# Attention on one core: the fourth query's block moved ahead of the first scores, one root for all queries' sums, and another order of output blocks and score groups

## What is computed

```python
def second_block(x, ...):
    h = rmsnorm(x, g_norm1[l]) * (1.0 + sc1) + sh1
    proj = h @ w_in[l]                                  # q 512, k 128, v 128, z 1024 columns
    q = apply_axial_rope(rmsnorm(q.reshape(B, S, 8, 64), g_q[l]), cos, sin)
    k = apply_axial_rope(rmsnorm(k.reshape(B, S, 2, 64), g_k[l]), cos, sin)
    s = einsum('bqkgd,bskd->bkgqs', q, k) / 8           # 8 query heads on 2 key heads
    attn = einsum('bkgqs,bskd->bqkgd', softmax(s), v)
    tok = chunked_token_mlp(z, g_tok_v[l], w_s[l], b_s[l])
    mixed = concatenate([rmsnorm(attn, g_attn_out[l]), rmsnorm(tok, g_tok_out[l])])
    x = x + gt1 * (mixed @ w_out[l])
```

## Time and profile before

| | |
|---|---|
| median of 3 runs | 737.29 us (737.09 to 738.39) |
| the profiled execution | 737.35 us, its span 735.4 us |
| PE busy | 721.1 us, 98% |
| DVE, ACT, POOL busy | 586.2, 469.0, 150.4 us |
| chain that ended last | PE 88%, DVE 4%, ACT 3% |

### The profile page before, as it was taken

One profiled execution on the slowest core, in us unless ns is written; L12 is line 12 of the kernel. 1 busy time (PEld: TensorE's weight loads), 2 busy tenths in 40 slices (PEclk: granted clock), 3 DMA queues, 4 the chain that ended last, 5 costly groups with the idle time before them and its releaser, 6 DMA issues.

```text
span 735.4 us, 14308 instructions
## 1 busy us (share of the span) xinstructions
PE 721.1 (98%) x5265; PEld 663.8 (90%) x5265; DVE 586.2 (80%) x880; ACT 469.0 (64%) x793; POOL 150.4 (20%) x151
## 2 busy tenths in 40 slices
PE   8999999999999999999999999999999999999996
PEld 7999999999999799888988877997889999999895
DVE  7999989855976587876686998998698889866667
ACT  7778775678765474555545548778686555555565
POOL 5000000021333042342232320010003121333330
PEclk9999999999999999999999999999999999999999
DMA  7664443354555859898787892963337775666551
GB/s 280 184 190 159 157 133 121 117 164 144 188 176 181 302 191 408 295 306 304 244 286 255 265 319 73 340 230 119 106 116 244 240 234 179 189 188 195 172 172 58
DMA packets 48082, 151.20 MB, mean 206 GB/s; under 512 B 9600, under 2 KB 11656, under 8 KB 48024
## 3 DMA queue, kind: packets, MB, share of 16 engines
q1 hardware_dynamic: 46184, 146.62, 60.0%
q10 hardware_dynamic: 1840, 3.80, 1.4%
HBM read 147.73 MB, written 1.06 MB: 202 GB/s over the span
## 4 chain that ended last, share of the span: by engine, by line
PE 88%; DVE 4%; ACT 3%; DMA 1%; issue 1%; SPq 1%; ACTq 0%; DVEq 0%
PE ps L881 30%; PE ps L538 21%; PE ps L814 21%; PE ps L1127 1%; PE ps L1187 1%; ACT wh L1241 1%; DVE wl L1856 1%; PE ps L669 1%; PE ps L1076 1%; DMA qrot<-qg 1%; PE ps L688 1%; PE ps L595 1%; DMA vtk<-in_x 1%; PE ps L954 1%; SPq L484 1%
## 5 line engine op out<-in xcount | busy, mean ns | idle before, releaser
L1856 DVE TENSOR_TENSOR wl<-raw,wh 128x1024 fp32r<-128x1024 f32 x220 | 282.6, 1291 | 78.9 <-ACT wh L1241 77.2
L1241 ACT ACTIVATE wh<-raw 128x1024 fp32r<-128x1024 f32 x220 | 231.5, 1055 | 62.4 <-PE ps L814 47.5
L881 PE MATMUL ps<-xh,wh 128*128 128x256 f32 x656 | 184.8, 282 | 0.0
L881 PE MATMUL ps<-xh,wl 128*128 128x256 f32 x656 | 183.8, 280 | 0.0
L881 PE MATMUL ps<-xl,wh 128*128 128x256 f32 x656 | 183.8, 280 | 0.0
L881 PEld LDWEIGHTS ps<-xh,wh 128*128 128x128 f32 x656 | 123.6, 188 | 3.8 <-issue 1.7
L881 PEld LDWEIGHTS ps<-xl,wh 128*128 128x128 f32 x656 | 123.5, 188 | 1.9
L881 PEld LDWEIGHTS ps<-xh,wl 128*128 128x128 f32 x656 | 123.7, 189 | 0.0
L538 PE MATMUL ps<-xh,wh 128*128 128x256 f32 (+2 forms) x400 | 116.9, 292 | 0.0
L538 PE MATMUL ps<-xh,wl 128*128 128x256 f32 (+2 forms) x400 | 113.2, 283 | 0.0
L538 PE MATMUL ps<-xl,wh 128*128 128x256 f32 (+2 forms) x400 | 113.0, 283 | 0.0
(11 more groups left out here) (443 smaller groups left out, 1244.6 us busy)
## 6 DMA issues: line engine op xcount, KB each, us to landing
raw<-in_w_stream SPq DMA_DIRECT2D x220, 512.0 KB, 3.9
ada_w<-in_w_ada SPq DMA_DIRECT2D x48, 512.0 KB, 6.1
vtk<-in_x SPq DMA_DIRECT2D x2, 512.0 KB, 4.6
tg_m<-in_ln_rows ACTq DMA_DIRECT2D x2, 512.0 KB, 7.1
out<-ob SPq DMA_DIRECT2D x4, 256.0 KB, 2.0
u<-uT SPq DMA_DIRECT2D x16, 34.0 KB, 2.5
eepp<-in_s_mats SPq DMA_DIRECT2D x1, 512.0 KB
decay_rows<-decay_dram SPq DMA_DIRECT2D x4, 128.0 KB
```

What stands on the lines that cost most here:

```text
L881: mm = nc.tensor.matmul(ps[:, bank, 0:SEQ], w, x, start=(k == 0), stop=(k == 3 * KD - 1))
L1241: nc.scalar.activation(wh[:, b % RING], raw[:, b % RING], ACT.Identity).then_inc(hi_done, 1)
L1856: V.tensor_tensor(wl[:, b % RING], raw[:, b % RING], wh[:, b % RING].bitcast(F32), ALU.subtract).then_inc(lo_done, 1)
```

## The change

Four things are reordered. (1) `scores(0)` no longer comes before input block n = 13 but after it, behind `q_stat(2)` and `q_stat(3)`. (2) ScalarE takes one root for the sums of all four queries in place of two, and takes block 13 out of PSUM before it and before the first `exps`. (3) On TensorE an output block stands between any two groups of scores, and turned probabilities, `weigh_v` and `turn_attended` come one output block later; `weigh_v(3)` comes behind output block 3 with none after it. (4) VectorE makes the token branch's low parts (L2542) and the second query before the first `maxima`, and the `lo` of output block 2 after them.

```diff
@@ q_stat, weigh_v (TensorE)
-                if i in (0, 2):
-                    pe.wait_ge(S["q_std"], i // 2 + 1)
-                if i == 2:
-                    pe.wait_ge(S["branch_std"], NT)
+                if i == 0:
+                    pe.wait_ge(S["q_std"], 1)
...
@@ TensorE, input blocks
                     q_stat(1)
-                    scores(0)
                 if n == 13:
                     q_stat(2)
-                    scores(1)
-                    turn_probs(0)
-                    turn_probs(1)
+                    q_stat(3)
+                    scores(0)
...
@@ TensorE, output blocks
                 mm.then_inc(blk_done, 1)
-                if n == 0:
-                    q_stat(3)
-                if n < 2:
-                    scores(n + 2)
                 if n < 3:
-                    turn_probs(2 * n + 2)
-                    turn_probs(2 * n + 3)
-                weigh_v(n)
+                    scores(n + 1)
+                turn_probs(2 * n)
+                turn_probs(2 * n + 1)
                 if n >= 1:
-                    turn_attended(n - 1)
+                    weigh_v(n - 1)
+                if n >= 2:
+                    turn_attended(n - 2)
+            weigh_v(QT - 1)
+            turn_attended(QT - 2)
...
@@ ScalarE
-            def q_std(first):
+            def q_std():
...
-                act.wait_ge(S["q_stat"], first + 3)
-                nc.scalar.activation(hb[:, 16 + 4 * first:24 + 4 * first], ps[:, 2, 256 + 4 * first:264 + 4 * first], ACT.Sqrt,
+                act.wait_ge(S["q_stat"], 1 + QT)
+                nc.scalar.activation(hb[:, 16:32], ps[:, 2, 256:272], ACT.Sqrt,
...
@@ VectorE, input block 13
                     mod_out(NMOD - 2, ADA_LOOP + 1, bank=5)
-                    q_scales(0)
+                    for m in range(QT):
...
+                    q_finish(2)
+                    q_scales()
                     maxima(0)
                     maxima(1)
-                    q_finish(2)
...
@@ VectorE, output blocks
-                if n == 1:
+                if n < 2:
                     q_finish(n + 3)
-                if n == 1:
-                    q_scales(2)
                 if n < 3:
                     maxima(2 * n + 2)
                     maxima(2 * n + 3)
-                if n == 0:
-                    q_finish(n + 3)
```

More of the change, by code:

```diff
@@ L1067, in weigh_v @@
                 if i == 0:
-                    pe.wait_ge(S["q_std"], 3)
+                    pe.wait_ge(S["q_std"], 2)
                     pe.wait_ge(S["branch_std"], NT)
@@ L1707, in _ @@
                         nc.scalar.activation(mh[:, QT + m, :], zu[:, m, :], ACT.Identity, scale=col("g_tok", m)).then_inc(S["branch_hi"], 1)
[L1708 to L1715, removed]
                 act.wait_ge(blk_done, b + 1)
@@ L1730, in _ @@
                         .then_inc(S["q_ev"], 1)
+                if n == 13:
+                    q_std()
+                    act.wait_ge(S["branch_ms"], 1)
+                    for t in range(NT):
+                        nc.scalar.activation(branch_rstd[:, t:t + 1], ps[:, 2, 300 + t:301 + t], ACT.Sqrt, bias=eps[:, 2:3], scale=2.0)\
+                            .then_inc(S["branch_std"], 1)
+                    exps(0)
+                    exps(1)
             for b in range(B_OUT2, B_F2):
@@ L1740, in _ @@
                     probt_copy(2 * n + 1)
-                if n == 0:
-                    q_std(2)
                 if n in (2, 3, 4, 5):
@@ L2454, in k_finish, with q_scales @@
                 V.tensor_tensor(dst, dst, qstd[:, 1, :], ALU.mult).then_inc(S["qk_ready"], 1)
-            def q_scales(first):
-                dve.wait_ge(S["q_std"], first // 2 + 2)
-                r = hb[:, 16 + 4 * first:24 + 4 * first]
+            def q_scales():
+                dve.wait_ge(S["q_std"], 2)
+                r = hb[:, 16:32]
                 step(V.reciprocal(r, r))
@@ L2523, in _ @@
                     mod_out(NMOD - 2, ADA_LOOP + 1, bank=5)
-                    q_scales(0)
+                    for m in range(QT):
+                        dve.wait_ge(S["branch_hi"], m + 1)
+                        V.scalar_tensor_tensor(ml[:, QT + m, :], zu[:, m, :], col("g_tok", m), mh[:, QT + m, :].bitcast(F32),
+                                               ALU.mult, ALU.subtract).then_inc(S["branch_lo"], 1)
+                    dve.wait_ge(S["mod_done"], ADA_LOOP + 1)
+                    step(V.scalar_tensor_tensor(gain[:, 1, :], mod[:, M_SC2:M_SC2 + KD], 1.0, span("g_norm2"), ALU.add, ALU.mult))
+                    q_finish(2)
+                    q_scales()
                     maxima(0)
                     maxima(1)
-                    q_finish(2)
-                    dve.wait_ge(S["mod_done"], ADA_LOOP + 1)
-                    step(V.scalar_tensor_tensor(gain[:, 1, :], mod[:, M_SC2:M_SC2 + KD], 1.0, span("g_norm2"), ALU.add, ALU.mult))
                 if n == 8:
@@ L2538, in _ @@
                     lo(B_IN2 + n + AHEAD)
[L2539 to L2543, removed]
                 if 2 <= n < KD:
```

## The result

The changed kernel takes **746.96 us** (median, 746.51 to 747.20) against 737.78 (737.09 to 738.39) for the kernel before on the same chip: ratio 1.0124, 95% interval 1.0111 to 1.0136, 9.2 us slower. 743.3 was forecast, 740.6 to 745.2 as the range. The profiled execution took 746.9, with a span of 745.0.

A forecast was written before the change was run, and what follows sets the result against it. The prediction took TensorE, with a chain of matmuls nearly throughout, to bound the kernel. Waits of 7.7 us added less 1.7 won gave +6.0, so 743.3 us, with a range of 740.6 to 745.2.

The forecast's parts named there:

- The clock falls: Rival: TensorE's granted clock drops after the 3.4 us idle before output block 2, adding up to 2.9: 746.2; chance 0.06.
- (c): Output block 2 waits for `part_done`, VectorE's steps from `attended(0)` to both `gated_part` lying bare: 3.4 us added.
- (d): The last `weigh_v` waits for `att_lo(1)`, whose bank it writes, with only `turn_attended(1)` as cover: 2.1 us added.
- (e): The attention branch's first block waits for the second `gated_part` (`part_done` at 4): 0.6 us added.
- (a): `q_stat(3)` waits for ScalarE to take input block 13 out: 0.5 us added.
- (b): `scores(1)` waits for `exps(1)`, 1.0 us added; `scores(2)` waits likewise, 0.1 us.
- What was won: Three TensorE waits, after `q_stat(2)`, after `q_stat(3)` and at `turn_probs`, go away: 1.7 us gained.
- The cap of 1.59: All TensorE idle time in the two profiled stretches, 1.59 us, limits what reordering can win by removing idle time.
- The table loads: ScalarE's two removed loads, 2 x 1.28 us, are worth nothing beyond the waits that go.
- absorbed: Rival: something later than TensorE, above all the weight stream, makes up the delay: 737.3 to 738.5; chance 0.08.
- The faster outcome: Rival: the exponentials' chain was the bound, (c), (d) and (e) are hidden, at best 735.7; chance 0.06.
- The wait at (d) doesn't vanish when (c) has one: Denies the rival that (c)'s wait lets ScalarE and VectorE run ahead, so (d) and (e) vanish: 740.6; chance 0.1.

The follow-up runs named there:

- busy_both: The changed kernel with matmuls of no use in TensorE's two long gaps, 11 before output block 2 and 7 before the last `weigh_v`, waits kept: 743.95 us, ratio 1.0082.
- before_gap_busy: The kernel before, with output block 2 also waiting for `att_lo(0)` and 11 matmuls of no use run meanwhile: 740.54 us, ratio 1.0045.
- gate1_early: The changed kernel with VectorE's first two `gated_part` moved ahead of the maxima of tile 2 and `attended(0)`: 742.13 us, ratio 1.0063.
- gate1_tail_best2: gate1_tail_qs with ScalarE's token-branch roots before block 13's evacuation and the scores' matmuls in order of heads: 737.05 us, ratio 0.9993.
- gate1_tail_qs: gate1_tail with `q_stat(3)` released by block 13's squares alone, not by the second evacuation behind them: 736.72 us, ratio 0.9989 to the kernel before.
- gate1_tail: gate1_early plus a reordered tail, the first attention block between the last two `weigh_v`, the last turns and `gated_part` pair moved along: 737.25 us, ratio 0.9994.
- before_gap: The kernel before with one wait added, output block 2 waiting for `att_lo(0)`, without fillers: 743.16 us, ratio 1.0073.
- busy_first: The changed kernel with only the first long gap, before output block 2, filled with matmuls of no use: 745.95 us, ratio 1.0110.
- gate1_busy: gate1_early with 7 matmuls of no use in the gap before the last `weigh_v`: 740.00 us, ratio 1.0030.

## Why the prediction was wrong, point by point

*The step that failed* is the price of the clock, put at nothing in the sum: the rival "The clock falls" was given 0.06 and left out of the sum and the range. The waits were right (7.7 forecast, 7.2 measured), but the likeliest case should have had on top what the slow matmuls cost, 2.25 + 1.7 = 3.95. busy_both and before_gap_busy show the cause: with the gap filled and the wait kept, the slow blocks are gone. The argument against it, a clock of 1.00, came from stretches whose gaps are 0.73 at most and bears on gaps of that length only. The prediction had itself written that "no row shows such a gap inside the program with the clock still up", and then gave that sentence no weight. The Trainium skill ("TensorE: Matmul & The Clock Gate", HAM oscillation), cited there, holds here: the granted clock of 0.50 behind (c)'s gap is its half rate.

*The rival's own size.* It priced one fall, behind (c), at up to +2.9. Measured are 2.25 there and 1.7 behind (d), a wait of 2.2 that the prediction costed at its own length only. So even this rival, 746.2, had one fall and not two. 743.3 + 2.25 + 1.7 = 747.3, less the (e) that the slow clock swallowed (0.6) is 746.7; measured 746.96.

*(a), (b), (c), (d)* each came within 0.15. (c)'s parts hold singly: free to `attended` 0.30 (0.27), to the `lo` 0.55 (0.55), to `gated_part` 1.14 (1.13), both of them 1.40, waking 0.10. VectorE had 1.10 to spare, where 0.9 was worked out. gate1_early shows that the order on VectorE was the cause: without `attended(0)` and the `lo` ahead, (c) is 0.

*(e)* was right about the chain and wrong about TensorE: the second `gated_part` ends at 532.16 + 0.74 = 532.90, but TensorE, at the low clock, was done only at 533.05. With the clock kept up the wait appears at 0.49 (busy_both), 0.57 forecast.

*What was won* is 1.9 against 1.7, the three waits (1.69) and 0.26 more at output block 1, which took 3.15 before (507.27 to 510.42) instead of 2.89. The cap of 1.59 that the prediction set on any such gain contradicts its own 1.7, and the measured gain is over it too: TensorE's busy time counts durations that reach over into the waits, so idle time taken from it comes out too small. The table loads gave nothing beyond, as forecast, and gate1_tail_best2 shows that even the remaining load isn't what `scores(1)` waits for.

*The other rivals.* The delay isn't absorbed (9.22 of the stretch, 9.2 of the medians). The faster outcome exists only with (c) and (d) both taken away (gate1_tail_qs), and then by 0.1%. The drain of 1.38 that this rival counted for a switch of tables isn't in the trace before: the root starts at 505.13, 0.02 behind the end of its load (503.83 + 1.28). The wait at (d) doesn't vanish when (c) has one.

## What to carry to other kernels

Before an order is changed, look on the other engines for what stands between the new producer and the instruction that TensorE will wait for: a step that used to be a block's length ahead (`weigh_v(0)`) put `attended`, a `lo` and two `gated_part` bare on the path, and moving those two ahead of it won 4.5 us. Where a gap of 2 us or more remains inside TensorE's work, count the wait and then 1 to 3 us again for the slow matmuls behind it, and try fillers: they took 2.1 to 2.5 and 2.6 us off two kernels with one such gap and 2.7 to 3.4 off the one with two. Read the granted clock in windows of a few us around each gap, since the page's slices average it away and a slow engine reads as busy.

## What the runs showed of the hardware

The clock fell behind a single gap of 1.98 us (gate1_early, 0.78 and 0.79 in two windows of 4), not only with those of 3.01 to 3.33. Behind the short gap it fell late: there TensorE had been back at work since 524.44, and windows of 0.5 us read 1.00 up to 526.0, 0.75 in the next and 0.50 from 526.5 to 529.5. Gaps of 0.50 and 0.74 (gate1_tail) left it at 1.00. How much a fall costs isn't fixed. Behind the long gaps block 2 took 2.25 and 2.37 (5.25 - 2.88, before_gap) longer. Behind the same gap of 1.98 it takes from `weigh_v(3)`'s start to `turn_attended(3)`'s 6.49 (after), 6.59 (gate1_early) and 7.98 (busy_first), against 5.32 with the clock kept up (busy_both, gate1_busy): 1.2, 1.3 and 2.7. These are net of the wait (e), 0.49, which appears only with the clock up; the 1.7 and 3.2 above are without that deduction. Which gaps between 0.8 and 2.0 are harmless wasn't tried.
